# RWKV block kernel: six unread bf16 products ahead of two waits of TensorE

## What is computed

```
def step(S, inp):
    r_t, w_t, k_t, v_t, kk_t, a_t = inp
    sa = jnp.einsum('bhvk,bhk->bhv', S, -kk_t)
    S = (S * w_t[:, :, None, :]
         + sa[..., None] * (kk_t * a_t)[:, :, None, :]
         + v_t[..., None] * k_t[:, :, None, :])
    y = jnp.einsum('bhvk,bhk->bhv', S, r_t)
    return S, y
```

## Time and profile before

| | |
|---|---|
| median of 3 runs | 2581.4 us (2577.13 to 2583.29) |
| profiled execution | 2584.5 us |
| its span | 2582.7 us |
| TensorE busy | 2364.1 us, 92% of the span |
| weight loads | 1528.9 us, 59% |
| VectorE, ScalarE, GpSimd busy | 792.0, 531.7, 576.5 us |
| mean granted clock of TensorE | 0.955 |
| RWKV stage | about 376 to 690 us of the span |

### The profile page before, as it was taken

One profiled execution on the slowest core, in us unless ns is written; L12 is line 12 of the kernel. 1 busy time (PEld: TensorE's weight loads), 2 busy tenths in 40 slices (PEclk: granted clock), 3 DMA queues, 4 the chain that ended last, 5 costly groups with the idle time before them and its releaser, 6 DMA issues.

```text
span 2582.7 us, 42530 instructions
## 1 busy us (share of the span) xinstructions
PE 2364.1 (92%) x18633; PEld 1528.9 (59%) x18633; DVE 792.0 (31%) x1724; ACT 531.7 (21%) x1097; POOL 576.5 (22%) x418
## 2 busy tenths in 40 slices
PE   8999997888789999999999997988889989899887
PEld 7888776767667664688888554433334444444442
DVE  4111315554545533232222343222221111111115
ACT  4111223342355512211111342000000000000002
POOL 5334333331111102433322111111111111111110
PEclk9999999998899999999999998989999999999999
DMA  4223110002110012211111627999999999999997
GB/s 195 88 93 128 74 74 28 27 13 87 64 66 2 1 69 71 89 41 57 58 41 33 258 77 284 422 429 429 429 419 419 429 429 429 429 430 429 429 429 317
DMA packets 73519, 536.86 MB, mean 208 GB/s; under 512 B 14104, under 2 KB 16408, under 8 KB 47600
## 3 DMA queue, kind: packets, MB, share of 16 engines
q1 hardware_dynamic: 58032, 505.97, 47.6%
q0 software_dynamic: 10240, 16.82, 1.7%
q10 hardware_dynamic: 5056, 11.28, 1.4%
HBM read 502.55 MB, written 43.52 MB: 211 GB/s over the span
## 4 chain that ended last, share of the span: by engine, by line
PE 74%; DMA 14%; DVE 5%; ACT 3%; issue 3%; POOL 0%; POOLq 0%; DVEq 0%; ACTq 0%; SPq 0%
PE banks L221 48%; DMA arena<-in_wg 13%; PE banks L226 8%; PE banks L228 8%; PE banks L227 8%; ACT arena L1604 1%; PE banks L2918 1%; ACT arena L231 1%; DVE arena L1583 0%; DVE arena L1129 0%; DVE arena L3222 0%; DVE arena L1149 0%; DMA h2d<-arena 0%; DMA arena<-in_con 0%; DMA arena<-in_wo 0%
## 5 line engine op out<-in xcount | busy, mean ns | idle before, releaser
L221 PE MATMUL banks<-arena 64*64 64x64 f32 (+12 forms) x15401 | 1686.4, 350 | 156.1 <-DMA arena<-in_wg 52.0
L221 PEld LDWEIGHTS banks<-arena 64*64 64x64 f32 (+4 forms) x15401 | 967.6, 156 | 814.0 <-issue 702.2
L231 ACT ACTIVATE arena<-banks 128x512 f32<-128x512 f32 (+5 forms) x317 | 181.7, 584 | 896.9 <-PE banks L221 581.7
L2912 POOL DMA_INDIRECT yb<-arena x64 | 64.8, 1012 | 787.8 <-DVE arena L3032 755.5
L3032 DVE TENSOR_SCALAR arena<-banks,arena 128x512 f32<-128x512 f32 x64 | 48.0, 751 | 500.5 <-PE banks L221 500.5
L226 PE MATMUL banks<-h1h,w2s 128*128 128x512 f32 x448 | 177.9, 397 | 1.7 <-DVE h1l L1969 1.7
L227 PE MATMUL banks<-h1l,w2s 128*128 128x512 f32 x448 | 175.4, 392 | 0.0
L228 PE MATMUL banks<-h1h,w2s 128*128 128x512 f32 x448 | 175.3, 391 | 0.0
L226 PE MATMUL banks<-hh,wlo 128*128 128x512 f32 x432 | 173.4, 401 | 0.0
L228 PE MATMUL banks<-hh,wlo 128*128 128x512 f32 x432 | 171.8, 398 | 0.0
L227 PE MATMUL banks<-hl,wlo 128*128 128x512 f32 x432 | 170.5, 395 | 0.0
(11 more groups left out here) (258 smaller groups left out, 1601.8 us busy)
## 6 DMA issues: line engine op xcount, KB each, us to landing
arena<-in_wg SPq DMA_DIRECT2D x64, 2048.0 KB, 31.1
arena<-in_wd SPq DMA_DIRECT2D x64, 2048.0 KB, 30.1
arena<-in_wu SPq DMA_DIRECT2D x63, 2048.0 KB, 25.7
arena<-in_w SPq DMA_DIRECT2D x55, 512.0 KB, 3.3
spill<-arena SPq DMA_DIRECT2D x27, 512.0 KB, 2.6
arena<-spill SPq DMA_DIRECT2D x27, 512.0 KB, 5.0
arena<-in_wo SPq DMA_DIRECT2D x16, 512.0 KB, 8.1
arena<-yb SPq DMA_DIRECT2D x8, 1024.0 KB, 13.0
```

The lines of the kernel that those rows point to most:

```text
L221: return pe.e.matmul(o, l, r, start=start, stop=stop)
L231: return act.e.activation(o, i, ACT.Copy)
L2912: return pool.e.indirect_dma_start(yb, bass.IndirectOffsetOnAxis(ap=six[:, col:col + 1].bitcast(U32), axis=0), src[:, :], None, bounds_che ...
```

## The change

A new helper `pe_awake` issues n products in bf16 of a 128x128 tile of the identity's bits with 512 columns of the mask's bits, into the first 512 columns of an opened bank. Their result is never read: the products that follow start with `start=True`. It is called with n = 6 at eleven places: ahead of the first F of each of the eight halves, and ahead of the first score of pairs 1, 2 and 3. At these places the bank is now opened first, then the six products are issued, and only then comes the wait for `A_first` and `T_first`, or for A, R, B and K.

```diff
+    def pe_awake(pe, t, n):
+
+        for _ in range(n):
+            pe.e.matmul(t[:, 0:512], C("id").bitcast(BF16)[:, 0:128], C("sc", 0, 256).bitcast(BF16), start=True, stop=True)
+
     def pe_F(pe, i, hf, lv, h):
         s_, c_, _, _ = LEVELS[lv]
         u = ps.open(pe, ("F", i, hf, lv, h), ring="main")
+        if (lv, h) == (0, 0):
+            pe_awake(pe, u.t, 6)
+            pe.wait_ge(s("A_first"), 2 * i + hf + 1)
+            pe.wait_ge(s("T_first"), 2 * i + hf + 1)
...
     def pe_main(pe, i):
         v, AR_, Bt_, Kt_, Dn_ = vq[i % 2], AR[i % 2], Bt[i % 2], Kt[i % 2], Dn[i % 2]
-        for name in ("A", "R", "B", "K"):
-            pe.wait_ge(s(name), i + 1)
         for hf in range(2):
             n_half = 2 * i + hf
             for g in range(2):
                 u = ps.open(pe, ("score", i, hf, g), ring="main")
+                if i and (hf, g) == (0, 0):
+                    pe_awake(pe, u.t, 6)
+                for name in ("A", "R", "B", "K"):
+                    pe.wait_ge(s(name), i + 1)
...
                 for h in range(2):
-                    if lv == 0:
-                        pe.wait_ge(s("A_first"), n_half + 1)
-                        pe.wait_ge(s("T_first"), n_half + 1)
-                    else:
+                    if lv:
                         w = ps["T", i, hf, lv - 1, h]
                         pe.wait_ge(w.free, w.v)
                     pe_F(pe, i, hf, lv, h)
```

## The result

The median went from 2581.8 us (2577.1 to 2583.3, four runs) to 2602.9 us (2601.6 to 2605.9, four runs): the ratio is 1.0086, with an interval of 1.0073 to 1.0099. That is 21 us slower, where +3 was forecast, and it lies outside the range (2577.5 to 2590.5). A second comparison later gave 1.0093 (1.0064 to 1.0121).

A forecast was written before the change was run, and what follows sets the result against it. It took TensorE's queue, where the stages follow each other, to set the end, with slow-clock stretches in the RWKV stage. 4.0 + 2.1 + 1.1 - 3.1 - 1.0 = +3.1 us gave 2584.5 us, range 2577.5 to 2590.5.

The forecast's parts named there:

- Nothing is queued differently on ScalarE, VectorE, POOL or SP; no DMA moves: Whole kernel: the closing claim before the sum, that the other engines' queues and DMA stay the same; given no cost.
- Second halves, -3.1 us: Inverse's first level, pairs 0 to 2: six products hide in TensorE's wait for POOL and hold the clock, about 1.0 us each.
- So only the ahead-of-VectorE part can shrink: Second halves: of 5.24 us to the next level, only the part before VectorE's L836 shortens, 1.0 us a place.
- First halves of pairs 0 to 2, +4.0 us: Inverse's first level: TensorE isn't waiting for POOL there, so the six show: 1.2, 1.4 and 1.4 us.
- First scores, +2.1 us: First scores of pairs 1, 2 and 3: the six are partly hidden by idle time, 0.7 us each.
- pair 3, +1.1 us: Pair 3's inverse: the six cost 0.7 us in the first half and 0.4 us in the second.
- May save one of them: Slow-clock stretches at 519.8 and 605.1 us, behind two instruction waits: the six may save one, -1.0 us.
- Rival 1: RWKV stage: the clock falls all the same; 7.2 us of cost and no gain, 2588.6 us; chance 0.20.
- Rival 2: RWKV stage: the clock is held much longer than at the five places, -7.0 us, 2574.4 us; chance 0.13.
- Rival 3: RWKV stage: the six are absorbed as later instruction waits shrink; sum about 0, 2581.5 us; chance 0.22.

The follow-up runs named there:

- the change with pads: The changed kernel plus 62 unread 32x32 products at the start of TensorE's queue, 256 added instructions in all; 1.0030 of the kernel before, +8 us.
- the one with 66 late: The kernel before plus 66 unread 32x32 products ahead of the first output projection, behind the RWKV stage; 1.0045 of the kernel before, +12 us.

## Why the prediction was wrong, point by point

**"Nothing is queued differently on ScalarE, VectorE, POOL or SP; no DMA moves": the step that failed.** The sentence left out TensorE's own stream. The 66 products put 132 instructions into it, and everything behind them lies elsewhere in the packets of 16 KB. The sum has no term for this; it was put at nothing without a reason. Measured by itself it is +14 us (1.0033 to 1.0077, that is +9 to +20); taken out of the change it leaves +8. The two make 22, for the 21 measured. The waits for instructions were in my rows, 2.88 and 2.11 us, and I read them as places that could hide a product. In each a packet lands, 1.38 and 1.28 us before TensorE goes on. I didn't ask what sets where they fall.

The Trainium skill (Runtime: NRT & Kernel Launch, Instruction fetch mechanics) says that an engine's instructions come in blocks of 16 KiB, which is 256 instructions, and that crossing a block is "mostly hidden". The packets of this trace have that size, and a shift of 256 cost nothing. "Mostly hidden" holds for most of the 149 packets but not for all: TensorE stood 2.88 and 2.11 us before the change, with no branch near, and 3.72 us behind the branch in the change. The measurement decides.

**Second halves, -3.1 us: mechanism half right, gain zero.** The six hid (TensorE then waited 1.16 us for POOL), the clock was held (1.00 for 0.50), and the first level's products took 1.16 us for 1.99. L836 could start 0.82 us earlier, near the 1.0 that I took. What failed is "So only the ahead-of-VectorE part can shrink", taken to shorten the path by 1.0. L836's length was treated as fixed at 2.18 us; it is 1.22 us of work and otherwise a wait for POOL's product, and became 2.95. The step to the next level, forecast at about 4.2 us, stayed at 5.20 for 5.25, and the runs gave +0.9 us for the set. With POOL held back it takes 3.46 us, so the cause is shown. The Trainium skill (SBUF — State Buffer, SBUF: two separate sides) has the rule: an operation of VectorE with two SBUF inputs and one of GpSimd take a shared pair of ports by an exclusive lock, whoever starts first for its whole instruction. The trace agrees: POOL's 2.36 us and then 1.08 us more make the 3.44. L832 too ends 1.08 us after POOL's L1178 beside it (484.48 to 485.56).

**First halves of pairs 0 to 2, +4.0 us: right in kind.** The step is 1.40 us in pair 1, and VectorE is 1.31 us to 1.55 us later behind the six there and 1.55 us in pair 2; in pair 0 it is only 0.4 to 0.7 us, where I took 1.2. The set alone, pair 3 with it, cost +2.6 us (0 to +5).

**First scores, +2.1 us, and pair 3, +1.1 us: a little low.** VectorE is 1.3 us later behind the six in pair 1's score and 1.7 to 2 us in pair 3's, for 0.7 taken at each. In pair 2 the wait for instructions, now 3.38 us, came just ahead of the six and hid none of them: they ran bare behind it for 2.09 us (525.46 to 527.55), as the clock fell to 0.50 there, for 0.7 taken. In pair 3's second half the step is 0.4 us, as taken. The set alone measured 0, so this didn't reach the end as such. I can't tell it from noise.

**"May save one of them", -1.0 us: no such gain.** The mean of the stage's clock is 0.92 over the 314 us, for 0.91 before and the 0.93 to 0.94 forecast. The low stretches moved rather than went.

**The rivals.** Rival 1 had no gain and 7.2 us of cost: with the shift taken out, +8 us is near its number. Its reason was wrong, since the clock didn't fall at the filled places; the gain was there and was lost to POOL. Rival 2 fell with the clock of 0.92 over the stage. Rival 3 had the stream in view with the wrong sign: more instructions gave no smaller waits, but one more wait at the end. My chances had no case in which the number of instructions matters, so the range was too narrow above.

**What stays open.** The final stage holds 4.4 to 6.0 us of the shift's cost. The other 8 to 10 us have no place in the traces. In the change they should lie in the RWKV stage, as at 740 us VectorE is 15.4 us late in it and 7.9 us late in the change with pads; but one profile differs from another by some 3 us there with nothing changed ahead of it (the one with 66 late), and the sum of TensorE's waits that end on "issue" didn't grow (18.5 us in 13 of them before and 12.7 us in 12 after, between 370 and 780 us). Why a shift of 132 brings two more packets (151 in all five such profiles) and one of 256 only one (150) isn't explained. Whether the clock's stretch near 467 us, at which VectorE falls behind by 1.46 us, belongs to the change or to that one execution wasn't settled either.

## What to carry to other kernels

Count the instructions that an edit adds, not only their time: in a long unrolled program a shift of TensorE's stream by half a packet cost twice what the products did, at places that nobody touched. Before you believe that a small edit is good or bad, run it with the same number of instructions doing nothing, and once filled up to 256. And before you put a gain on an engine's next operation, look at what runs beside it on POOL: if its length changes with another engine's start, it is a wait. And where an idle time of TensorE ends on nothing, look for a branch in its queue and for a packet of instructions landing.

## What the runs showed of the hardware

- Shifting TensorE's stream by 132 instructions costs 1.0055 (1.0033 to 1.0077) of the time; by 66 it costs 0.9997 (0.9988 to 1.0007), by 256 it costs 1.0004 (0.9990 to 1.0019). The extra wait at the final stage lasts 2.6 to 4.4 us and stands in five profiles of five with the shift of 132, in none of the other fifteen.
- A branch of TensorE took 6.37 us in its queue, before and after, and TensorE then stood idle for 3.40 and 3.43 us.
- A product of two 128x1024 f32 tiles took VectorE 1.22 us with POOL out of the way, 2.17 to 2.95 us beside one of POOL's, and ended 3.43 or 3.44 us after POOL's start in each case. The same holds the other way: POOL's addition of 128x512 took 1.28 us alone and 2.25 us beside such a product of VectorE's.
- Six unread bf16 products of 512 columns kept the clock at 1.00 over the next 3.5 us at three places out of three; with six of 32 columns it was at 0.50 at two of the three and fell soon behind the third. Over the stage the mean rose from 0.91 to 0.92 only.
